# A two-layer hybrid encoder: the mixes' low parts computed on GpSimd instead of VectorE

## The reference

```python
h = modulate(rms(x, norm1_g[1]), sh1, sc1)
xx = pad(h, one step)[:, :-1] - h              # the token before, less this one
mix = lambda idx: h + xx * mu[idx]             # six of them
r, k, v = (mix(0) @ w_r, mix(1) @ w_k, mix(2) @ w_v)
w = -softplus(-(w0 + tanh(mix(3) @ w1) @ w2)) - 0.5
a = sigmoid(a0 + (mix(4) @ a1) @ a2)
g = sigmoid(mix(5) @ g1) @ g2
```

## Time and profile before

| | us |
|---|---|
| median of 3 runs | 3121.45 |
| lowest and highest of them | 3116.18, 3122.15 |
| the profiled execution | 3126.26 |
| its span in the profile | 3124.5 |
| TensorE busy in it | 2800.0 |
| VectorE, GpSimd, ScalarE busy | 1582.2, 1399.3, 977.5 |

### The profile page before, as it was taken

One profiled execution on the slowest core, in us unless ns is written; L12 is line 12 of the kernel. 1 busy time (PEld: TensorE's weight loads), 2 busy tenths in 40 slices (PEclk: granted clock), 3 DMA queues, 4 the chain that ended last, 5 costly groups with the idle time before them and its releaser, 6 DMA issues. The chain is left out here.

```text
span 3124.5 us, 58516 instructions
## 1 busy us (share of the span) xinstructions
PE 2800.0 (90%) x25184; PEld 2314.8 (74%) x25184; DVE 1582.2 (51%) x1939; ACT 977.5 (31%) x1703; POOL 1399.3 (45%) x742
## 2 busy tenths in 40 slices
PE   1787898999999999898978988888659999999999
PEld 1565676888877887677767887888647888878887
DVE  6744545656536343679635555555313543333344
ACT  2434433222232222445433333333224222222221
POOL 2532244444445444434435555656236444444443
PEclk9889999999999999999989999999879999999999
DMA  6421233544423232465651111111042222222223
GB/s 232 162 74 34 89 128 114 175 162 173 163 82 104 85 101 95 112 166 137 168 142 57 50 54 53 50 50 50 24 120 95 81 101 98 97 95 94 97 99 122
DMA packets 208642, 327.19 MB, mean 105 GB/s; under 512 B 126209, under 2 KB 126337, under 8 KB 208385
## 3 DMA queue, kind: packets, MB, share of 16 engines
q1 hardware_dynamic: 208384, 323.44, 32.5%
HBM read 288.86 MB, written 33.55 MB: 103 GB/s over the span
## 5 line engine op out<-in xcount | busy, mean ns | idle before, releaser
L687 POOL TENSOR_TENSOR wl<-w,wh 128x1024 fp32r<-128x1024 f32 x368 | 905.9, 2468 | 1305.0 <-ACT wh L728 1304.8
L180 PE MATMUL ps<-hi,wh 128*128 128x512 f32 x2208 | 883.8, 400 | 57.4 <-POOL wl L687 42.6
L181 PE MATMUL ps<-lo,wh 128*128 128x512 f32 x2208 | 870.0, 394 | 0.0
L182 PE MATMUL ps<-hi,wl 128*128 128x512 f32 x2208 | 869.5, 394 | 0.0
L728 ACT ACTIVATE wh<-w 128x1024 fp32r<-128x1024 f32 x368 | 388.1, 1056 | 708.3 <-DMA w<-in_ffn_w_in 527.7
L180 PEld LDWEIGHTS ps<-hi,wh 128*128 128x128 f32 x2208 | 420.4, 190 | 159.8 <-POOL wl L687 42.8
L994 DVE SCALAR_TENSOR_TENSOR xt<-ps,mod,xt 128x512 f32<-128x512 f32 x384 | 286.4, 750 | 437.7 <-PE ps L182 437.4
L181 PEld LDWEIGHTS ps<-lo,wh 128*128 128x128 f32 x2208 | 420.7, 191 | 89.5 <-issue 3.7
L182 PEld LDWEIGHTS ps<-hi,wl 128*128 128x128 f32 x2208 | 420.1, 190 | 90.0
L180 PE MATMUL ps<-act_hi,wh 128*128 128x512 f32 x704 | 282.2, 401 | 18.2 <-DVE act_lo L1003 9.7
L999 DVE TENSOR_TENSOR act<-ps,silu 128x512 f32<-128x512 f32 x88 | 60.8, 691 | 467.2 <-PE ps L182 467.2
(11 more groups left out here) (209 smaller groups left out, 3805.4 us busy)
## 6 DMA issues: line engine op xcount, KB each, us to landing
w<-in_ffn_w_in SPq DMA_DIRECT2D x176, 512.0 KB, 3.4
piece<-in_ada_w SPq DMA_DIRECT2D x96, 512.0 KB, 4.8
w<-in_ffn_w_out SPq DMA_DIRECT2D x88, 512.0 KB, 3.3
w<-in_w_rkv SPq DMA_DIRECT2D x48, 512.0 KB, 3.8
scratch<-silu SPq DMA_DIRECT2D x48, 256.0 KB, 2.9
scratch<-act SPq DMA_DIRECT2D x48, 256.0 KB, 2.9
w<-in_wqk SPq DMA_DIRECT2D x20, 512.0 KB, 5.0
xt<-in_xT SPq DMA_DIRECT2D x4, 2048.0 KB, 10.8
```

The costliest lines, as they stand in the source:

```text
L180: pe.matmul(out, w_hi(k), x_hi(k), start=first and k == 0, stop=False)
L181: pe.matmul(out, w_hi(k), x_lo(k), start=False, stop=False)
L182: ins = pe.matmul(out, w_lo(k), x_hi(k), start=False, stop=last and k == kc - 1)
L687: pool.tensor_tensor(wl[n % NW][:, :, :], wr[n % NW][:, :, :], wh[n % NW][:, :, :].bitcast(F32), ALU.subtract).then_inc(*wlo.up)
```

## The change

The step "low" of every mix is taken out of VectorE's program and put into GpSimd's, with the same operands, the same wait for `mix_hi` and the same signal `mix_lo`. The plan and its order are the same. So the low parts stand in GpSimd's queue where their step stands in the list, between its splits of weight tiles.

```diff
@@ GpSimd's program
+                            elif step == "low":
+                                q, = e
+                                h, mix, k, fresh, reader = plan.mixes[q]
+                                pool.wait_ge(*mix_hi.at(q + 1))
+                                pool.tensor_tensor(mixed(lo, al, h, mix, k), tn[q % 2][:, :], mixed(hi, ah, h, mix, k).bitcast(F32),
+                                                  ALU.subtract).then_inc(*mix_lo.up)
                             elif step == "lsplit":
@@ VectorE's program
-                            elif step == "low":
-                                q, = e
-                                h, mix, k, fresh, reader = plan.mixes[q]
-                                dve.wait_ge(*mix_hi.at(q + 1))
-                                dve.tensor_tensor(mixed(lo, al, h, mix, k), tn[q % 2][:, :], mixed(hi, ah, h, mix, k).bitcast(F32),
-                                                  ALU.subtract).then_inc(*mix_lo.up)
```

## The result

| | kernel before | changed kernel |
|---|---|---|
| median of 4 runs, us | 3121.8 | 3165.95 |
| lowest and highest | 3116.18, 3122.86 | 3164.36, 3166.86 |
| ratio | | 1.0143, 95% interval 1.013 to 1.0155 |
| span of the profiled execution, us | 3124.5 | 3163.9 |

The change makes the kernel slower by 44 us, or 1.4%. The forecast was 3155 us, slower by 34, with a range of 3132 to 3180: the direction and the mechanism hold, the size was a quarter short.

A forecast was written before the change was run, and what follows sets the result against it. TensorE, busy for 2800.0 of 3124.5 us, bounds the kernel; in the projections it waits for VectorE, which Pool blocks. Terms 5.4 + 5.4 + 9.1 + 10 + 2 + 2 = 33.9 on 3121.5 give 3155 us, range 3132 to 3180.

The forecast's parts named there:

- the shared resource: In the second layer's projections VectorE operations on two SBUF operands and Pool's take turns, 1.69 us for one of each.
- The pair's ring: Two mixes (next product's, LoRA's) through VectorE, ScalarE, Pool and back: 3.52 us becomes 4.25, with a weight tile 6.35.
- The 4.4: The ring of a pair if the lock is held for the instruction's whole 1.27 us: 4.4 instead of 4.25 us.
- Product 0: First of six second-layer projection products (half n // 3, projection n % 3): +9.1 us, bounds 5 and 16.
- The term of the squares: In product 0, Pool's additions of squares for the next norm, ScalarE waiting: about 0.4 us for each of seven, +3.
- Products 2 and 5: Product 2's first part and product 5, single mixes with every gap: eight lows 0.58 us longer each, +2 us each.
- The +2.8: Product 2 into product 3: norm's steps wait for the last low part, eight more mixes at +0.35 to 0.5 each.
- The FFN's tail: First layer's FFN: eight low parts before weight tiles TensorE already waits for, +2 us, bounds 0 and 4.
- The clock: TensorE's clock falls to half after some longer waits; hidden while the ring is the slower, so nothing added.
- (a): Rival: the engines don't shut each other out, pair 4.1 us under TensorE's 4.33, waits go: 3105 us, chance 0.06.
- (c): Rival, lockstep: three engines wait in order, ring 5.0 and more, TensorE also waits for wl: 3175 to 3185, chance 0.13.
- (b): Rival: no change, TensorE's lead takes up the longer ring: 3123 us, chance 0.07.

The follow-up runs named there:

- the spare subtractions: Kernel before plus, beside each low part, a 128x512 subtraction on Pool of constants into a buffer nobody reads: ratio 1.026, 3208.0 us against 3126.1.
- the run with the pairs alone: Changed kernel with only the 64 low parts of mixes 1 to 4 on Pool, the others on VectorE: ratio 1.0077, 3149.8 us against 3126.1.
- the run with the singles: Changed kernel with only the 32 low parts of mixes 0 and 5 on Pool: ratio 1.0051, 3143.2 us against 3126.1.

## Why the prediction was right, and where it was short

**What bounds the kernel, and the shared resource: right.** The turns of 1.69 us, read from three additions of squares beside VectorE's operations, came back in the changed kernel: two low parts of 1.74 and 1.75 us that start 1.69 apart. The kernel with the spare subtractions shows that no dependency is needed for them.

**The pair's ring: right.** 4.41 us measured for 4.25, 6.26 for 6.35. Products 1 and 4 were given 5.4 and have 4.7 and 4.5, product 3's own part 5.1 and has 5.6 (by the run with the pairs alone). The 4.4 that the prediction names for a lock over the whole instruction is no better forecast: it leaves out the 0.25 us until the next high part is there, and with it that sum is 4.6, above the measured 4.41. For the pairs with a tile the turns are one reason and not the only possible one: with the low parts on Pool and the tiles on VectorE such a pair is 5.84 us long by the order of the queues and the waits in them. The ring is slow by the sum of what stands in its three engines' queues, and the turns are one of the things in it. (The sum of the lower bounds, with products 1 and 4 worked out for a ring of 4.0, is 17 and not 16.)

**Product 0: +9.1, measured +11.2.** The start was nearly right: +1.9, where TensorE's first wait is 2.04 us instead of 0.52. The term of the squares was too small: +3 for seven additions, where some 5 are left when the start and the pairs' 4.2 are taken off (an estimate by difference). ScalarE in product 0:

```profile
1293.57 0.63 ACT L822 ACTIVATE sq<-xt 128x512 f32<-128x512 f32 x1 [5.61 <-POOL squares L700]
```

It waits 5.61 us for the additions, which stand behind two low parts on Pool, and the next high parts stand behind this wait on ScalarE. A later round ends in TensorE's longest wait. The low part that it waits for had its high part at 1303.9, but a weight tile and two additions stood in front of it on Pool until 1307.9:

```profile
1310.42 0.80 PE L180 MATMUL ps<-act_hi,lora_wh 128*128 128x512 f32 x1 [5.83 <-POOL act_lo L715]
```

**Products 2 and 5: +2 each, measured +5.8 and +6.0.** This is the one step that was wrong in kind. It and product 0 came out 9.9 us too small together, and the table's whole gap is 8.3. The +2.8 for what product 2 hands on to product 3 has 2.3 in the run with the singles. The prediction counted 0.58 us more for each low part "partly in time in which VectorE waits", and did not look at what stands in front of each low part in Pool's order; the weight tile in front of the third was in that order, and the 8.22 us for which Pool waited before it in the kernel before was in the trace. The run with the tile behind the low part takes the term down to 1.1.

**The FFN's tail: +2, measured +1.8.** TensorE's two waits of 2.95 and 2.09 us are 3.73 and 4.04 now, 2.7 us more. The term itself is no larger than what executions differ by, so this one hit proves little.

**The clock.** The prediction added nothing for it, since the ring was to be the slower of the two. In products 1 and 4 that is so: at their longest waits (3.43 and 3.44 us) the granted clock falls for 3.4 us, and still TensorE waits again at the next first-stage LoRA matmul (0.23 and 0.17 us). In product 3 it falls at 1500.2, and TensorE waits 2.13 us at 1511.6. In products 2 and 5 it is not: from the matmul at 1625.73, behind a wait of 2.45 us, the twelve matmuls up to the next LoRA matmul of the first stage take 4.45 us where the same ones took 2.75 before, and the granted clock is at the lower of its two levels, 1.2 GHz, for 3.4 us of it. So about 1.7 us of product 5's 6.0 are matmuls at that level, with the wait in front of them.

**The rivals.** (a), faster, wanted the two engines not to shut each other out; the spare subtractions show that they do. With an operation of 0.62 us in the same place the pairs do get closer together than before (4.67 us for 5.16 in product 1). (c), lockstep, is near what happened in product 0, whose pairs are 7.23 us apart (5.86 before); but no wl is among TensorE's releasers in the products, as (c) wanted. (b) is out: every product has its loss.

## What to carry to other kernels

Before moving an operation to an engine with idle time, write down the ring that it lies in (who waits for whom, until the first waits again) and add what it gains, what it displaces on a shared resource, and every instruction that stands in front of it in the new engine's queue with its own wait. Busy shares said that Pool had half of its time free here; the ring said that it would be the one waited for. And where one engine blocks another by turns, look at the blocker's own wait as well as its length (here 2.40 us on Pool, 1.23 on VectorE): the same move was worth nothing at one place in the queue and 0.5% one gap later.

## What the runs showed of the hardware

- VectorE's operations on two SBUF operands and Pool's operations shut each other out even when they touch different tiles: both at 128x512, one of each takes 1.67 to 1.81 us from one start to the next in the changed kernel, where alone they take 0.69 and 1.27. This is also so for a Pool operation that nobody waits for.
- The same operation of VectorE with one operand in PSUM is not held up. In the trace of the kernel before, 384 additions of the residual (L994, 128x512) are spread over the whole kernel; 99 of them lie at least nine tenths within a Pool instruction, nearly all of these weight tiles, and take 751 ns in the median, as do the 209 that meet none. Of the 96 mixes, of the same shape with both operands in SBUF, the 58 that meet none take 751 ns in the median too; the 32 that overlap with one in part take 1760, and the 6 that lie within one 2778.
- Pool's copy of 128x512 (0.62 us) takes half of its subtraction (1.27 us), and beside a VectorE operation it is 1.08 us long.
